# First modulation by output columns, its weight blocks stationary with 32 moving columns, and the first gated products started with the first slice

## The reference, cut to what matters

```python
mod = silu(c) @ w_mod[l] + b_mod[l]              # 6 sections of 1024 columns
sh1, sc1, g1, sh2, sc2, g2 = split(mod, 6)
mod_ctx = silu(c_ctx) @ w_mod[l] + b_mod[l]      # its first two sections are used
h  = rms_norm(x, norm_mix_w) * (1 + sc1) + sh1   # x: 1024 tokens x 1024 channels
hc = rms_norm(ctx, norm_mix_w) * (1 + sc1c) + sh1c   # ctx: 256 tokens
proj = h @ w_in                                  # 768 columns q, k, v; 1024 gated (GLU)
u = ga * sigmoid(gb)                             # then a 31-tap depthwise convolution
```

## Time and profile before

| | |
|---|---|
| median of three runs | 1183.94 us |
| profiled execution | 1190.29 us, span 1188.4 us |
| PE busy | 1128.5 us, 95% of the span |
| DVE busy | 937.2 us, 79% |
| ACT busy | 577.2 us, 49% |
| POOL busy | 296.4 us, 25% |
| DMA | 171.77 MB, mean 145 GB/s |

### The profile page before, as it was taken

One profiled execution on the slowest core, in us unless ns is written; L12 is line 12 of the kernel. 1 busy time (PEld: TensorE's weight loads), 2 busy tenths in 40 slices (PEclk: granted clock), 3 DMA queues, 4 the chain that ended last, 5 costly groups with the idle time before them and its releaser, 6 DMA issues.

```text
span 1188.4 us, 17094 instructions
## 1 busy us (share of the span) xinstructions
PE 1128.5 (95%) x5953; PEld 959.4 (81%) x5953; DVE 937.2 (79%) x1422; ACT 577.2 (49%) x991; POOL 296.4 (25%) x337
## 2 busy tenths in 40 slices
PE   7899999899998999998799999999999999999995
PEld 7687888799888887876688888787888878888884
DVE  0579988779997754469999999999999966877763
ACT  1662356766556764455343434343443534444441
POOL 2200111135454000002555454545510020000111
PEclk9999999999998999999899999999999999999998
DMA  9422556529999315222545454545433284543574
GB/s 364 159 75 77 120 107 117 145 46 257 245 240 277 107 46 170 86 88 90 159 127 180 135 171 131 171 129 175 136 111 106 91 307 159 118 114 98 125 160 62
DMA packets 103090, 171.77 MB, mean 145 GB/s; under 512 B 9322, under 2 KB 62690, under 8 KB 102004
## 3 DMA queue, kind: packets, MB, share of 16 engines
q1 hardware_dynamic: 82388, 104.70, 26.7%
q0 software_dynamic: 20640, 66.27, 23.9%
HBM read 112.21 MB, written 31.46 MB: 121 GB/s over the span
## 4 chain that ended last, share of the span: by engine, by line
PE 37%; DVE 13%; issue 7%; ACT 5%; DVEq 0%; ACTq 0%; POOL 0%
PE ps L1684 14%; PE ps L1734 6%; PE ps L1736 6%; PE ps L1735 6%; PE ps L1649 5%; DVE y L2100 3%; DVE w_op L2001 3%; DVE w_raw L2019 2%; DVE y L2096 2%; ACT w_op L1805 2%; ACT y L1893 1%; DVE u L2089 1%; DVE s_sum L2019 1%; ACT h_second L1798 0%; PE ps L1660 0%
## 5 line engine op out<-in xcount | busy, mean ns | idle before, releaser
L1684 PE MATMUL ps<-t_op,w_op 128*128 128x512 f32 x1056 | 247.5, 390 | 2.5 <-issue 0.9
L1684 PEld LDWEIGHTS ps<-t_op,w_op 128*128 128x128 f32 x1056 | 197.9, 188 | 46.0 <-issue 2.9
L1684 PE MATMUL ps<-hx,w_op 128*128 128x512 f32 x792 | 192.0, 396 | 9.6 <-DVE u L2089 7.0
L1684 PEld LDWEIGHTS ps<-hx,w_op 128*128 128x128 f32 x792 | 151.0, 191 | 43.3 <-DVE u L2089 6.5
L1805 ACT ACTIVATE w_op<-w_raw 128x512 fp32r<-128x512 f32 x132 | 79.9, 623 | 193.8 <-DVE w_raw L2019 191.6
L1734 PE MATMUL ps<-dnh,ah 128*128 128x512 f32 x308 | 120.1, 390 | 1.6 <-DVE dnl L2107 1.6
L1735 PE MATMUL ps<-dnl,ah 128*128 128x512 f32 x308 | 119.8, 389 | 0.0
L1736 PE MATMUL ps<-dnh,al 128*128 128x512 f32 x308 | 119.8, 389 | 0.0
L2001 DVE TENSOR_TENSOR w_op<-w_raw,w_op 128x512 fp32r<-128x512 f32 x132 | 102.5, 791 | 9.8 <-ACT w_op L1805 7.7
L1913 ACT ACTIVATE ah<-hid 128x512 fp32r<-128x512 f32 x77 | 48.6, 631 | 116.8 <-PE ps L1736 112.8
L2107 DVE TENSOR_TENSOR al<-hid,ah 128x512 fp32r<-128x512 f32 x77 | 53.3, 692 | 48.8 <-ACT ah L1913 48.1
(11 more groups left out here) (293 smaller groups left out, 2392.2 us busy)
## 6 DMA issues: line engine op xcount, KB each, us to landing
w_raw<-in_w_up SPq DMA_DIRECT2D x44, 512.0 KB, 5.1
wm<-in_w_mod SPq DMA_DIRECT2D x32, 512.0 KB, 6.4
sums<-wm POOLq DMA_DIRECT2D x32, 512.0 KB, 8.1
wd<-in_w_down POOLq DMA_DIRECT2D x44, 256.0 KB, 3.4
w_down_sums<-wd POOLq DMA_DIRECT2D x44, 256.0 KB, 2.8
dn_raw<-w_down_sums SPq DMA_DIRECT2D x44, 256.0 KB, 2.6
hid_scratch<-hid SPq DMA_DIRECT2D x20, 512.0 KB, 4.4
hid<-hid_scratch POOLq DMA_DIRECT2D x20, 512.0 KB, 5.2
```

The source lines that it names most:

```text
L1684: last = pe.matmul(bank_of(p, s), w_op[p][w][:, k, :], rows_of(p, k, v), start=(start and k == 0 and w == 0 and v == 0), stop=(k == KH - 1 ...
```

## The change

Only the first stage and the hand-over to the later gated groups are edited.

- `wm` is loaded by output columns: block k holds columns 128 k to 128 k + 127 of the shift and of the scale section, all 1024 input channels (two loads of 512 KB, each of 1024 runs of 512 B). From block 4 on a load waits on PE's block k - 4.
- `modulate(k)` runs 16 products with 32 moving columns and yields shift and gain of channel block k alone. The results alternate between banks 6 and 7. DVE's `modulation(k)` takes two small operations for each k.
- SP's order is now: four token tiles, block 0, gated weight 0, block 1, gated weight 1 (in a buffer of its own), block 2, two tiles, block 3, two tiles, blocks 4 to 7, context.
- POOL issues the norm weight and b_mod first, between its first constants; the other vectors wait until these two have landed. Their transposes go to bank 3 and their copies on DVE come after k = 1.
- PE interleaves: at step k the first half of group 0, `modulate(k+2)`, the first half of group 1 for k - 1, and `x_item(k+2)`. The second halves of groups 0 and 1 are interleaved too, with the last five items.
- The four context transposes move from group 1 to group 2, their copies on ACT too, and `hcx` moves from group 2 to group 3.

```diff
-        wm = at(143, "wm", [P, KT, 2 * D])
+        wm = at(143, "wm", [P, KT, 2, KT, P])
-        natw = at(127, "natw", [P, KT, P])
+        QW = P // 4
+        natw = at(127, "natw", [P, KT, QW])
+        gw_raw1 = at(83, "gw_raw1", [P, KT, P])
...
                 def load_mod(k):
-                    sp.dma_start(wm[:, k, :], w_mod[0, k * P:(k + 1) * P, 0:2 * D]).then_inc(wm_in[WM_SEM[k][0]], 16)
+                    if k >= 4:
+                        sp.wait_ge(mod_mm, k - 3)
+                    for j in range(2):
+                        c0 = j * D + k * P
+                        sp.dma_start(wm[:, k, j], w_mod[0, :, c0:c0 + P].rearrange("(kc p) n -> p kc n", p=P)).then_inc(wm_in[k % 4], 16)
...
+                pool.wait_ge(vec_in, 32)
                 for v, r0, n, src in parts:
...
+                def modulate(k):
+                    pe.wait_ge(wm_in[k % 4], 32 * (k // 4 + 1))
+                    if k >= 2:
+                        pe.wait_ge(ab_done, 2 * (k - 1))
+                    for j in range(2):
+                        for kc in range(KT):
+                            last = pe.matmul(ps[:, mod_bank(k), j * QW:(j + 1) * QW], wm[:, k, j, kc, :], natw[:, kc, :],
+                                             start=(j == 0 and kc == 0), stop=(kc == KT - 1), skip_group_check=True)
                     last.then_inc(mod_mm, 1)
...
-                for k in range(KT):
-                    mod_item(k)
-                    if k == 4:
-                        vectors()
-                for n in range(NXB):
-                    x_item(n)
+                for k in range(2):
+                    modulate(k)
+                    x_item(k)
+                vectors()
                 pe.wait_ge(gw_lo, 1)
                 for k in range(KT):
                     pe.wait_ge(h_lo, k + 1)
                     glu_half(0, 0, k)
+                    if k + 2 < KT:
+                        modulate(k + 2)
+                    if k == 1:
+                        pe.wait_ge(gw_lo, 2)
+                    if k:
+                        glu_half(1, 0, k - 1)
+                    x_item(k + 2)
+                x_item(KT + 2)
+                glu_half(1, 0, KT - 1)
                 for k in range(KT):
                     pe.wait_ge(h_lo, KT + k + 1)
                     last = glu_half(0, 1, k)
+                    if k == KT - 1:
+                        last.then_inc(gl_mm, 1)
+                    if k + 3 < KT:
+                        x_item(KT + k + 3)
                     last = glu_half(1, 1, k)
                 last.then_inc(gl_mm, 1)
...
+                        if n == 2 and k >= KT // 2:
+                            ctx_item(k - KT // 2)
...
+                def modulation(k):
+                    dve.wait_ge(mod_mm, k + 1)
+                    dve.tensor_tensor(out=mod_both[:, :, :, k], in0=ps[:, mod_bank(k), 0:2 * QW].rearrange("p (j w) -> p w j", j=2)[:, 0:2, :],
+                                      in1=bias_cols[:, :, k].unsqueeze(1).to_broadcast([P, 2, 2]), op=ALU.add).then_inc(ab_done, 1)
+                    dve.scalar_tensor_tensor(out=gain_both[:, :, k], in0=mod_both[:, :, 1, k], scalar=1.0,
+                                             in1=cols[:, C_NMIX + k:C_NMIX + k + 1].to_broadcast([P, 2]), op0=ALU.add, op1=ALU.mult).then_inc(ab_done, 1)
...
+                for k in range(KT):
+                    modulation(k)
+                    if k < 2:
+                        split_glu(k)
+                    if k % 2:
+                        h_full_item(k)
+                    h_low(k)
+                    if k == 1:
+                        vector_columns()
+                    if k == 3:
+                        mean_squares(1)
+                    if k == 4:
+                        inverse_rms(1)
+                for n in range(KT, NXI, 2):
                     h_full_item(n + 1)
                     h_low(n)
                     h_low(n + 1)
```

More of the change, by code:

```diff
@@ L352, in build @@
             x_in = [sem1(f"x_in{t}") for t in range((TT + CT) // 2)]
-            wm_in = [sem1(f"wm_in{i}") for i in range(6)]
+            wm_in = [sem1(f"wm_in{i}") for i in range(4)]
             const_step, const_done = sem1("const_step"), sem1("const_done")
@@ L449, in load_mod @@
                 def load_mod(k):
-                    sp.dma_start(wm[:, k, :], w_mod[0, k * P:(k + 1) * P, 0:2 * D]).then_inc(wm_in[WM_SEM[k][0]], 16)
+                    if k >= 4:
[3 more added lines that the diff above has]
+                        sp.dma_start(wm[:, k, j], w_mod[0, :, c0:c0 + P].rearrange("(kc p) n -> p kc n", p=P)).then_inc(wm_in[k % 4], 16)
                 def load_glu(n):
-                    sp.dma_start(gw_raw[:], win[:, :, glu_col(n):glu_col(n) + P]).then_inc(gw_in, 16)
-                for k in range(KT - 1):
-                    load_mod(k)
+                    raw, landed = (gw_raw1, gw1_in) if n == 1 else (gw_raw, gw_in)
+                    sp.dma_start(raw[:], win[:, :, glu_col(n):glu_col(n) + P]).then_inc(landed, 16)
                 for t in range(TT // 2):
                     load_x(t)
-                load_mod(KT - 1)
+                load_mod(0)
                 load_glu(0)
-                for t in range(TT // 2, TT):
+                load_mod(1)
+                load_glu(1)
+                load_mod(2)
+                for t in (4, 5):
                     load_x(t)
-                sp.wait_ge(gw_lo, 1)
-                load_glu(1)
+                load_mod(3)
+                for t in (6, 7):
+                    load_x(t)
+                for k in range(4, KT):
+                    load_mod(k)
                 for t in range(CT):
@@ L505, in _ @@
                 pool.memset(ident[:], 0.0).then_inc(const_step, 1)
+                pool.dma_start(vec_b[0:KT, :], rows(norm_mix_w[0], KT)).then_inc(vec_in, 16)
+                pool.dma_start(vec_b[KT:7 * KT, :], rows(b_mod[0], 6 * KT)).then_inc(vec_in, 16)
                 pool.memset(maskf[:], 0.0).then_inc(const_step, 1)
@@ L558, in _ @@
                 pe.transpose(ps[:, 7, 0:2 * KT], cvecs[0:2 * KT, :], ident[0:2 * KT, 0:2 * KT]).then_inc(vecT, 1)
+                pe.wait_ge(vec_in, 32)
+                pe.transpose(ps[:, 6, 2 * KT:9 * KT], vec_b[0:7 * KT, :], ident[0:7 * KT, 0:7 * KT]).then_inc(vecT, 1)
                 def vectors():
[L561 to L565, removed]
+                    pe.wait_ge(vec_in, 32 + vec_total)
+                    off = C0
+                    for v, n in enumerate((N_A - C0, 4 * FT, 4 * FT, TAPS * CTL)):
+                        last = pe.transpose(ps[:, 3, off:off + n], vecs[0:n, v, :], ident[0:n, 0:n])
                         off += n
@@ L594, in ctx_item @@
                     last.then_inc(xT, 1)
-                def mod_item(k):
-                    pe.wait_ge(wm_in[WM_SEM[k][0]], 16 * WM_SEM[k][1])
+                def modulate(k):
+                    pe.wait_ge(wm_in[k % 4], 32 * (k // 4 + 1))
                     if k == 0:
                         pe.wait_ge(silu_done, 3)
-                    for j in range(2 * KT):
-                        last = pe.matmul(ps[:, j // 4, j % 4 * P:(j % 4 + 1) * P], wm[:, k, j * P:(j + 1) * P], natw[:, k, :],
-                                         start=(k == 0 and j % 4 == 0), stop=(k == KT - 1), skip_group_check=True)
+                        pe.wait_ge(cols_done, 1)
+                    if k >= 2:
[4 more added lines that the diff above has]
+                                             start=(j == 0 and kc == 0), stop=(kc == KT - 1), skip_group_check=True)
                     last.then_inc(mod_mm, 1)
@@ L892, in _ @@
                 split_glu(0)
[L893 to L902, removed]
-                split_glu(1)
-                for n in range(KT, NXI):
+                h_item(0)
+                split_glu(1)
+                h_item(1)
+                h_item(2)
+                square(4)
+                square(5)
+                h_item(3)
+                square(6)
+                square(7)
+                root(1)
+                for n in range(4, NXI):
                     h_item(n)
@@ L914, in _ @@
                         split_qkv(n - 1)
-                    if n == 1:
+                    if n == 2:
                         for i in range(4):
@@ L1103, in split_glu @@
                     dve.wait_ge(gw_hi, n + 1)
-                    dve.tensor_tensor(out=gwl[:, n % 2], in0=gw_raw[:], in1=f(gwh[:, n % 2]), op=ALU.subtract).then_inc(gw_lo, 1)
+                    dve.tensor_tensor(out=gwl[:, n % 2], in0=(gw_raw1 if n == 1 else gw_raw)[:], in1=f(gwh[:, n % 2]), op=ALU.subtract).then_inc(gw_lo, 1)
                 def split_qkv(k):
@@ L1111, in _ @@
                 dve.tensor_copy(natw[:].rearrange("p k (r two) -> p k r two", two=2),
-                                nat.unsqueeze(2).to_broadcast([P, KT, P // 2, 2])).then_inc(silu_done, 1)
+                                nat.unsqueeze(2).to_broadcast([P, KT, QW // 2, 2])).then_inc(silu_done, 1)
```

(14 more changed lines are left out.)

77 lines of the change are left out of this document (32 added, 45 removed).

## The result

The changed kernel took 1214.28 us in the median of four runs (1207.66 to 1227.03), the kernel before 1184.37 us beside it. The ratio is 1.0213, with a 95% interval of 1.0162 to 1.0264: some 25 us slower, where 1186 us and no measurable change were forecast. 1214 us lies above the forecast range of 1174 to 1197 us. The slowest of the four runs, 1227.03 us, is left out of the ratio.

A forecast was written before the change was run, and what follows sets the result against it. PE, busy 95% of the span, was taken as the bound, with DVE's taps as tight. T = 12.7 + 56.9 + 1.7 + 2.5 + 0.6 = 74.4 us shifts group 5 by +2.3 us, giving 1186 us; range 1174 to 1197 us.

The forecast's parts named there:

- Modulation on PE: First stage: eight blocks of 32 records at 0.107 us each take 27.4 us, 4.1 us less than before.
- Rival 1: Clock stays at 1.2 GHz where narrow products fill PE's time: about +20 us, +40 us at worst; chance 0.13.
- the late start: Front: PE can begin modulation only when block 0 has landed, at 12.7 us.
- the 2.5 us of stalls: First halves of groups 0 and 1: PE awaits block 3 for 1.55 us and block 4 for 0.95 us.
- T: Moment at which PE ends the second halves of groups 0 and 1, forecast at 74.4 us.
- clock and load terms: Additions up to T: 1.7 us lost to a start at 1.2 GHz, 2.5 us of waits for blocks.
- the forecast's main case: Whole kernel: front gains eaten by slower loads, late start and hand-over; +2.3 us, 1186 us; chance 0.50.
- Loads: Front: modulation blocks in 512 B runs move at 296 GB/s, 3.54 us a block instead of 2.6.
- Rival 2: Modulation loads in 512 B runs reach line rate, no load stalls: shift -1.2 us, 1183 us; chance 0.17.
- Rival 4: Modulation loads slower than the first gated weight showed, 5 us a block: +10.4 us, 1194 us; chance 0.10.
- Hand-over: Before group 2: PE waits 3.8 us for weights split after group 0, then loses 1.7 us at low clock.
- Carried on: From T to group 5: PE's and DVE's lists both give a shift of T - 72.1, +2.3 us.

The follow-up runs named there:

- E4: The changed kernel with 128 moving columns in modulation blocks 0 and 1 and 32 in blocks 2 to 7: 1212.64 us, ratio 1.0221 to the kernel before.
- E1: The changed kernel with 128 instead of 32 moving columns in each modulation product, nothing else different: 1192.82 us, ratio 1.0052 to the kernel before.
- E5: E1 with the second half of group 0 taken whole before that of group 1: ratio 1.0047 to the kernel before.
- E3: The kernel before with 32 instead of 128 moving columns in its modulation products, order and loads untouched: 1210.36 us, ratio 1.0193.
- E6: The kernel before with 64 instead of 128 moving columns in its modulation products: ratio 1.0201.
- E7: The kernel before with 96 instead of 128 moving columns in its modulation products: ratio 0.9991.

## Why the prediction was wrong, step by step

**Modulation on PE: the step that failed.** The term of 27.4 us measured 42.3 us. The price of 0.107 us a record holds, nearly, at the full clock only. It was taken from 16 records that stood between wider work, and I let the whole stream have it. Rival 1 named the mechanism and its place, and got 0.13. The argument that set it aside, that each step holds 1.4 us of 512-column products, is what E4 refutes. Its size was between the two figures given (+20 for half of the stretch, +40 at worst). By E1 the width alone moves group 2 by 18 us, from 82.59 to 100.54 us; the 5.4 us that remain against the kernel before (77.17 us) are the late start, the loads and the hand-over. Why narrow records leave the clock low isn't shown.

The gain that was set against it, 4.1 us, was misread as well. The 0.123 us of the kernel before is a mean over its own start at the low clock; its last 96 records went at 0.112 us. E4's block 2 shows the narrow form at 0.113 us, so at the full clock there was almost nothing to win. And the 14 us at the low level from which rival 1 was said to decide don't follow from the prediction's figures: half is lost there, so the 9.5 us still missing to 1% and the 2.5 us of stalls need 24 us.

**How T came out.** PE ended the second halves at 96.5 us instead of 74.4, which is T; group 2 starts 4.04 us later. Without the clock and load terms the forecast was 12.7 + 56.9 + 0.6 = 70.2 us; the difference is 26 us, nearly all of it the low clock, behind which the waits for loads vanished. From their starts to those of what follows, the eight blocks took 42.3 us instead of 27.4, 14.9 us; most of the other 11 or so lie in the wide products and transposes that shared the low clock, which the forecast's main case priced at the full clock. With the clock kept (E1) T was 78.6 us, still 4.1 above the forecast: 0.4 from the start, 1.3 from the blocks, 0.7 from waits, and 1.7 in products and transposes, each priced a little low.

**Loads: right in price, late by 2 us.** Block 0's products began at 12.93 us (12.7 forecast), and in E1 PE waited 2.9 us for blocks 3 and 4 (2.5 forecast). They came at 31.6 and 37.9 us where 29.4 and 35.6 were forecast; as PE was late by as much, the waits agree partly by luck. Runs of 512 B moved at 278 to 299 GB/s at 12 to 16 us, as the one early row said, not at the 403 GB/s of the long runs. In the change itself PE waited for no block after the first, as it was slower than the loads. Rival 2 is out, and with it, for this load, the figure of 512 B for line rate in the Trainium skill's "DMA: Bandwidth & Descriptors", Specifications. Rival 4 is out too.

**Hand-over: right in place and size.** 3.8 us of wait were forecast, 4.04 us are there, in the change and in E1, with the low clock behind it. It was rated as eating a gain; E5 shows that taking it away shifts the wait to DVE's items.

**Carried on: right.** T - 72.1 gives 24.4 us at group 5; the trace has 25.7. The break-even T of 72.1 us, where DVE's taps and PE meet, explains why E1, with T = 78.6 and a forecast of +6.5 us, is 8.0 us later at attention and 1.0052 in time.

**The page on the clock.** Rival 1 leaned in part on the Trainium skill's "TensorE: Matmul & The Clock Gate", Part 4, that transposes do not count as activity. E3 has hardly a transpose in 55 us and was low throughout, so for this loss the page's rule was not the reason; the narrow products themselves were.

## What to carry to other kernels

Before narrowing a matmul's moving side, ask what else holds TensorE's clock in that stretch: columns that compute nothing useful can pay for themselves, here by 18 us. A price per instruction from a short burst is a price at the clock of its neighbours, so look for a stretch as long as the one planned, and if there is none give the low clock an even chance. And when work is interleaved so that all of a group ends at the end, look at what was hidden behind its old, earlier end.

## What was not expected of the hardware

- The clock column reads 1.00 although records run at half speed: up to 50 us in the changed kernel, and in E3 and E6.
- With 32 columns the level swings in a period of about 7 us, the high level during narrow products and the low one during wide ones that follow (windows above).
- In one and the same order (E3, E6, E7, and the kernel before) 32 and 64 moving columns ran at 0.214 us a record, 96 and 128 at 0.112 to 0.129 us.
- Most of the difference between two executions in the attention stage is time at 1.2 GHz and PE's idle time, so a single trace says little about changes of a few microseconds elsewhere.
